# Prompt attention scores as three products of split halves instead of one full float32 product

## The reference, cut to what matters

```python
c_q, c_kv, kr_raw, g_a, x_b, g_b, q_m, g_m = split_cols(x @ w_in, EVEN_SPLITS)
q = (rms_norm(c_q, q_norm) @ w_uq).reshape(B, T, H_A, QK_NOPE + QK_ROPE)     # 8 heads, 64 + 32
q_lat = jnp.einsum('bthn,chn->bhtc', q[..., :QK_NOPE], w_uk)
q_rope = jnp.transpose(rope(q[..., QK_NOPE:], pos), (0, 2, 1, 3))
latent = rms_norm(c_kv, kv_norm)
k_rope = rope(kr_raw[:, :, None, :], pos)[:, :, 0, :]
...
s = (q_lat . latent + q_rope . k_rope) * MLA_SCALE       # causal, blocks of 128 queries
p = softmax(s);  o_lat = p @ latent;  y_a = o_lat @ w_uv
mixed = concatenate([y_a * silu(g_a), h_b * silu(g_b), y_m * silu(g_m)])   # h_b: RG-LRU, y_m: memory attention
```

## Time and profile before

| | us |
|---|---|
| median of 3 runs | 1392.4 |
| lowest and highest | 1391.83, 1393.7 |
| profiled execution, own time | 1393.73 |
| its span | 1392.1 |
| PE busy in the span | 1364.4 (98%) |
| DVE busy | 814.5 (59%) |
| ACT busy | 591.9 (43%) |
| mean granted clock of TensorE | 0.994 of full speed |

### The profile page before, as it was taken

How to read it: one execution, slowest core, us unless ns; L and a number is a source line. 1 busy time by engine, 2 the same in 40 slices (tenths; PEclk the granted TensorE clock), 3 DMA queues, 4 the chain that set the end, 5 groups by cost and what they waited for, 6 DMA issues and landing times.

```text
span 1392.1 us, 24975 instructions
## 1 busy us (share of the span) xinstructions
PE 1364.4 (98%) x10020; PEld 1236.3 (89%) x10020; DVE 814.5 (59%) x1541; ACT 591.9 (43%) x1062; POOL 116.9 (8%) x215
## 2 busy tenths in 40 slices
PE   9999999999999999999999999999999999999996
PEld 9988999787767667689998898999999999999996
DVE  4487753175675766756984344325444649545786
ACT  4169622156566565533552333115443135212453
POOL 1000000010001305600002000010000010000000
PEclk9999999999999999999999999999999999999998
DMA  6211133210003057745665311124334120124562
GB/s 215 63 31 46 31 112 103 75 43 14 1 1 124 15 144 224 204 146 181 211 201 188 107 31 43 61 62 66 61 61 115 31 107 31 48 68 154 172 217 94
DMA packets 59300, 135.77 MB, mean 98 GB/s; under 512 B 9001, under 2 KB 37898, under 8 KB 58418
## 3 DMA queue, kind: packets, MB, share of 16 engines
q1 hardware_dynamic: 48882, 112.45, 25.2%
q0 software_dynamic: 10160, 21.56, 6.5%
q10 hardware_dynamic: 144, 0.18, 0.0%
HBM read 120.65 MB, written 13.50 MB: 96 GB/s over the span
## 4 chain that ended last, share of the span: by engine, by line
PE 83%; DVE 7%; issue 5%; ACT 3%; POOLq 1%; DMA 0%; POOL 0%; DVEq 0%; ACTq 0%
PE ps L578 14%; PE ps L580 13%; PE ps L579 13%; PE ps L710 5%; PE ps L712 5%; PE ps L711 5%; PE ps L1153 3%; PE ps L1190 2%; PE ps L1165 2%; PE ps L1327 2%; PE ps L591 1%; PE ps L3278 1%; PE ps L3273 1%; DVE ln_sq L981 1%; DVE w_lo L526 1%
## 5 line engine op out<-in xcount | busy, mean ns | idle before, releaser
L578 PE MATMUL ps<-x_hi,w_hi 128*128 128x352 f32 x1288 | 425.7, 331 | 0.0
L580 PE MATMUL ps<-x_hi,w_lo 128*128 128x352 f32 x1288 | 415.0, 322 | 0.0
L579 PE MATMUL ps<-x_lo,w_hi 128*128 128x352 f32 x1288 | 414.5, 322 | 0.0
L578 PEld LDWEIGHTS ps<-x_hi,w_hi 128*128 128x128 f32 x1288 | 242.8, 189 | 9.7 <-issue 9.0
L579 PEld LDWEIGHTS ps<-x_lo,w_hi 128*128 128x128 f32 x1288 | 243.7, 189 | 1.0 <-issue 1.0
L580 PEld LDWEIGHTS ps<-x_hi,w_lo 128*128 128x128 f32 x1288 | 242.7, 188 | 0.0
L520 ACT ACTIVATE w_hi<-w_raw 128x1024 fp32r<-128x1024 f32 (+1 forms) x105 | 121.2, 1154 | 239.9 <-PE ps L580 132.3
L526 DVE TENSOR_TENSOR w_lo<-w_raw,w_hi 128x1024 fp32r<-128x1024 f32 (+1 forms) x105 | 141.1, 1344 | 61.9 <-ACT w_hi L520 61.5
L710 PE MATMUL ps<-mx_hi,w_hi 128*128 128x352 f32 x480 | 155.5, 324 | 0.3 <-issue 0.2
L712 PE MATMUL ps<-mx_hi,w_lo 128*128 128x352 f32 x480 | 154.5, 322 | 0.0
L711 PE MATMUL ps<-mx_lo,w_hi 128*128 128x352 f32 x480 | 154.0, 321 | 0.0
(11 more groups left out here) (515 smaller groups left out, 2003.0 us busy)
## 6 DMA issues: line engine op xcount, KB each, us to landing
w_raw<-in_w_out SPq DMA_DIRECT2D x48, 640.0 KB, 3.8
w_raw<-in_w_in SPq DMA_DIRECT2D x57, 512.0 KB, 3.6
page<-in_cache_mla SPq DMA_DIRECT2D x128, 128.0 KB, 2.5
kvs<-in_mem_cache SPq DMA_DIRECT2D x16, 512.0 KB, 4.8
x_res<-in_xT SPq DMA_DIRECT2D x24, 176.0 KB, 2.4
x<-x_next POOLq DMA_DIRECT2D x3, 1408.0 KB, 7.9
x_res<-x SPq DMA_DIRECT2D x24, 176.0 KB, 2.3
w_mem<-in_w_mem SPq DMA_DIRECT2D x2, 2048.0 KB, 10.6
```

Of the source, the lines that this page charges most:

```text
L578: pe.matmul(out, w_hi[:, (u + 1) % 2, kk], x_hi[:, k, chunk(c)], start=(k == 0), stop=False)
L579: pe.matmul(out, w_hi[:, (u + 1) % 2, kk], x_lo[:, k, chunk(c)], start=False, stop=False)
L580: mm = pe.matmul(out, w_lo[:, (u + 1) % 2, kk], x_hi[:, k, chunk(c)], start=False, stop=(k == KX - 1))
```

## The change

Scores are made of halves as the projections are. ScalarE rounds a unit's 128 columns of `qT` to `q_hi` (`query_hi`), VectorE subtracts (`query_lo`), and PE adds three products of type float32r. `query_hi` and `query_lo` of the units in `ISSUE[n+1]` stand in step n of their engines. The keys are kept as `kT_hi` and `kT_lo`. For the first pair VectorE makes `kT_lo` from PSUM; for the later pairs ScalarE first copies the whole piece into the buffer `rq` and makes `kT_hi` from there, and VectorE makes `kT_lo` from there. The rotated key is now made in input slots 60 and 61, with PSUM banks 5 to 7 as scratch, and PE's first pieces wait for it. `kT_lo` takes the place of `mx` tiles 4 to 7, which are written to memory after 233 us and read back behind the load of `w_uv`, ahead of the pages of the second half. Two small loads (`w_if`, the second mask) move to the end of the attention.

```diff
+        kT_hi = keep("kT_hi", [P, 4, T], F32R)
+        kT_lo = place("kT_lo", [P, 4, T], M0 + 4 * ROWS, F32R)
...
-                pe.wait_ge(rope_ready, u.h + 1)
+                pe.wait_ge(prep_ev, PAIR_PIECE[u.h // 2] + 5)
+                pe.wait_ge(kl_ready, 2 + 2 * u.h if u.h < 2 else KL_DONE[u.h // 2])
...
+                pe.wait_ge(ql_ready, HEAD_UNIT[n] + 1)
+                qh, ql = split_q_of(n)
+                w = u.nk // parts_of(u)
+                for a in range(parts_of(u)):
+                    s, ks = ps[:, u.bank + a, 0:w], (u, a * w, a * w + w)
+                    pe.matmul(s, qh, k_of(kT_hi, *ks), start=True, stop=False)
+                    pe.matmul(s, qh, k_of(kT_lo, *ks), start=False, stop=False)
+                    mm = pe.matmul(s, ql, k_of(kT_hi, *ks), start=False, stop=True)
...
+            def query_hi(n):
...
+                act.wait_ge(rope_ready, h + 1)
...
+                elif i >= 3:
+                    act.wait_ge(sc_ready, HEAD_AT[i - 3] + 1)
+                act.activation(split_q_of(n)[0], q_of(UNITS[n]), ACT.Copy).then_inc(qh_ready, 1)
...
             for n in range(len(UNITS)):
                 for k in ISSUE[n]:
                     maxima(k)
+                for k in ISSUE.get(n + 1, ()):
+                    query_lo(k)
                 invert(n)
                 if part_done_at(n) is not None:
                     into_mx(part_done_at(n))
...
+            def query_lo(n):
...
+                dve.wait_ge(qh_ready, HEAD_UNIT[n] + 1)
+                dve.tensor_tensor(lo, q_of(UNITS[n]), hi, ALU.subtract).then_inc(ql_ready, 1)
...
+                    if what == "k" and i >= N_FIRST:
+                        act.wait_ge(kl_ready, KL_DONE[p - 1] + (p == 2))
+                        act.activation(rq[:, cols], bank(b), ACT.Copy).then_inc(prep_ev, 1)
+                        act.wait_ge(prep_ev, i + 1)
+                        for r in range(2):
+                            act.activation(kT_hi[64 * r:64 * r + 64, s + r, cols], rq[64 * r:64 * r + 64, cols],
+                                           ACT.Copy).then_inc(kh_ready, 1)
+                        return
...
+        def dve_rope_key(dve, v, step):
+            part = ps[0:ROPE, 5:8, 0:CH]
+            if step == 0:
...
+                v.then(dve.stream_shuffle(raw, raw, swap))
+                v.then(dve.tensor_tensor(raw, raw, rope_sin[0:ROPE, :], ALU.mult))
+                dve.tensor_tensor(raw.rearrange("p (c n) -> p c n", c=NCH), raw.rearrange("p (c n) -> p c n", c=NCH),
+                                  part, ALU.add).then_inc(kr_ready, 1)
...
+            if s in (60, 61):
+                dve_rope_key(dve, v, s - 60)
...
+                sp.dma_start(mx[:, 4:8, :], mxd).then_inc(tbl_in, 16)
...
+            gp.wait_ge(lru_mul, 4)
+            gp.dma_start(mxd, mx[:, 4:8, :]).then_inc(spill, 16)
...
+            pe.wait_ge(kr_ready, 3)
             for i in range(N_FIRST - 1):
```

More of the change, by code:

```diff
@@ L242, in build @@
         rec2 = keep("rec2", [P, 2, P])
-        rec4 = [[place("rec4_00", [P, P], S0 + 7296), place("rec4_01", [P, P], S0 + 7808)],
-                [place("rec4_10", [P, P], X0 - 512), place("rec4_11", [P, P], at["rec2"])]]
-        assert at["rq"] <= S0 + 7296 and at["rec4_01"] <= S0 + 2 * ROWS
+        rec4 = [place("rec4_0", [P, P], X0 - 512), place("rec4_1", [P, P], at["rec2"])]
+        q_at = (at["kT_lo"], Z0 + 14 * ROWS + 4096, Z0 + 14 * ROWS + 4608, S0 + 7296, S0 + 7808, at["masks"] - 512)
+        q_hi = [place(f"q_hi{n}", [P, P], q_at[2 * n], F32R) for n in range(3)]
+        q_lo = [place(f"q_lo{n}", [P, P], q_at[2 * n + 1], F32R) for n in range(3)]
+        assert at["rq"] <= S0 + 7296 and at["q_lo1"] <= S0 + 7808 and at["q_hi0"] <= M0 + 8 * ROWS
         wh = place("wh", [P, 2, 7 * P], W0)
@@ L1108, in probs_of @@
             return probs[:, n % 2, 0:u.nk]
+        HEAD_AT = [n for n, u in enumerate(UNITS) if u.h is not None]
         FILLS, fill = {}, 0
@@ L1243, in act_attention, with dve_attention @@
                 evacuate(n)
-        def dve_attention(dve, v, between):
+        def dve_attention(dve, v, between, query_lo):
             def maxima(n):
@@ L1269, in invert @@
                     v.then(dve.reciprocal(mst[:, b, M_REC, :], mst[:, b, M_SUM, :]))
+                    last = max((g for g in range(PART_OF[n]) if PARTS[g].p is None), default=None)
+                    if last is not None:
+                        dve.wait_ge(o_ready, last + 1)
                     for t in range(2):
[L1271 removed]
+                        ins = dve.tensor_copy(rec4[t][:, :].rearrange("p (r d) -> p r d", r=2),
                                               mst[:, b, M_REC, 2 * t:2 * t + 2].unsqueeze(2).to_broadcast([P, 2, 64]))
@@ L3214, in _ @@
                 rope_sum(h)
-            rope_keys(2)
-            rope_keys(3)
-            v.settle()
-            dve_attention(dve, v, rope_at)
+            for h in range(2):
+                for i in (6, 7):
+                    keys_lo(i, h)
+                query_lo(h)
+            dve_attention(dve, v, rope_at, query_lo)
             dve_mla_sample(dve, v)
```

178 lines of the change are left out of this document (119 added, 59 removed).

## The result

The changed kernel takes 1433.5 us (median of 4 runs, 1432.04 to 1435.98) against 1392.3 us before: ratio 1.0296, 95% interval 1.0282 to 1.0311. It is 41 us slower where 27 had been forecast. The profiled execution lies at the median.

The account below looks back on a forecast made before the run. The prediction took PE to bound the kernel, busy 1364.4 of 1392.1 us. Its terms, -11.3 + 32.5 - 3 + 6 + 2.9 and 0 for memory, summed to +27.1 us: a median of 1419.5 us, range 1403 to 1433.

Parts of the forecast that it names:

- A: Attention scores on PE: three products of halves replace the full product, -11.3 us, bounds -9 to -12.
- B: Attention: PE waits for VectorE's `query_lo` before a unit's scores, late at 33 of 46 points, +32.5 us.
- C: Correction to the `query_lo` waits: VectorE catches up where its own backlog made it late, -3 us, between 0 and -10.
- D: New work on the keys, on VectorE and ScalarE, ahead of maxima and `query_lo`: +6 us, between 0 and +14.
- a rival: Attention: the clock falls after PE's many waits, adding 10 to 20 us, total 1430 to 1440 us; chance 0.09.
- E: Entry to the attention: PE waits for the rotated key, and the first scores start later, +2.9 us.
- F: Way of `mx` over memory, read back behind `w_uv` ahead of later pages: 0, range 0 to +5 us.
- the count of late points: Attention: `query_lo` comes too late for PE's scores at 33 of 46 points, VectorE in time at 13.
- The premise under A: Attention: PE binds, busy 215.43 of 222.20 us, so less PE work shortens it one for one if nothing takes its place.

Follow-up runs that it names:

- e4: Changed kernel plus useless transposes of the identity on PE ahead of its waits at units 9, 27, 51 and 52; 1424.5 us.
- e2: Changed kernel without `query_lo`; the third product takes `q_hi` again, so the scores lack a term; 1396.6 us.
- e3: Changed kernel with one full float32 score product again, without `query_hi` and `query_lo`, keys and entry kept as changed; 1400.2 us.
- e9: e7 with the product of `q_hi` and `kT_lo` left out, two products instead of three; 1399.0 us.
- e7: Changed kernel with `query_hi` and `query_lo` both one step earlier, two steps ahead, on their own engines; 1398.6 us.
- e8: e7 with PE's rotated-key wait at its second piece, pair 1's rotated-key copy and subtraction on GpSimd, two `rope_sum` two steps later; 1400.0 us.
- e10: e7 with PE's rotated-key wait at its second piece, `rope_sum` two steps later, GpSimd's zeros moved away from VectorE's copies; 1395.3 us.
- e12: e10 with all `query_lo` moved from VectorE to GpSimd, still two steps ahead; 1395.3 us.
- e11: Changed kernel with only GpSimd's zeros moved away from VectorE's copies of the rotated key; 1432.8 us.

## Why the prediction was wrong

The direction was right, and so was the mechanism of the waits; what the waits do to the clock was not, and the size of A was off. The 39.8 us of the two spans, by the steps of the prediction:

| step | forecast | measured | from |
|---|---|---|---|
| A, PE's work on scores | -11.3 | -6.4 | 8 sizes of unit, start to start |
| B, C, D, waits for `query_lo` | +35.5 | +36.8 | 32 places |
| slow clock in the stage | 0 (a rival) | +10.4 | windows |
| PE's other waits in the stage | 0 | -3.5 | 14.5 to 11.0, start to start |
| E, entry | +2.9 | +3.0 | 1.5 at the first piece, 1.5 to the first score |
| F, sample stage | 0 | +1.0 | 97.3 to 98.3 us |
| ahead of the first piece, behind the sample stage | 0 | +2.3, -1.6 | start of the same instructions |

They sum to 42.0, and the four of the stage to 37.3 where it grew by 35.0; this 2.2 us I can't assign. The slow clock is the least certain of them: filling the long waits in e4 took 7.0 us of it away and made the stage 6.1 us shorter. The -1.6 us in the last row is a stretch at the lower clock at 1105 us of the trace of before that the changed kernel's doesn't have.

**The step that failed is the sum's treatment of the clock.** It stood in the sum at nothing and was set apart as a rival of 0.09 at 1430 to 1440 us, with the argument that waits of this size had left the clock at 1.00 before. But before the longest wait in the stage was 1.2 us; the forecast's own list had waits of 2.3 us. The changed kernel's stage has 10.4 us of slow clock. e4 shows what the waits do: with the four longest filled, 7.0 us of it and 6.1 us of the stage are gone; in e2, without them, there is none, though PE waits 2.4 us for ScalarE there once. That the time lies in the rival's range is partly luck: the rival had a fifth of the stage at the lower level, the trace has a tenth (24 of 257 us), and A came out 4.9 us short. Also, the forecast spoke of "up to 2.3 us and more" but took no account of where the new work on the keys falls together with other work ahead of one `query_lo`: unit 9 (two key subtractions, the rotated key's copy and subtraction, two maxima) waited 3.9 us and unit 27 (two key subtractions and a `rope_sum` of 1.25 us) 3.0 us. D was spread over the steps in the forecast; these two places are where it gathers.

**A was mis-sized.** A unit of 1024 keys takes 1.47 us and not 1.35: 0.075 us is the first product behind other work of PE, with or without a wait, and the pace of 512 columns is 0.23 us and not 0.225. Over the eight sizes a head takes 6.9 us, not 6.3. Where the Trainium skill (TensorE: Matmul & The Clock Gate, Back-to-back issue gap) has 131 ns for a matmul of 512 columns in a stream, this trace shows 230 ns; its price would have been further off than mine.

**B, C and D held as a sum, to 1.3 us, and E to 0.1 us,** and so did the count of late points (32 for 33) and the first scores' 1.5 us behind the first piece. C and D can't be told apart in the traces, so that each was right is not shown. That the whole entry lies 2.3 us later than that is no part of the change's own work: 0.76 us are there after 24 us, and 1.5 us come at 119 to 124 us, where PE ran at the lower clock behind a wait of 1.81 us that left it alone in the kernel before (1.85 us, clock 1.00).

**The premise under A holds only so far.** "Less work on PE would shorten it one for one" was read from PE being busy 215 of 222 us. From e3 to e2, with the same keys and no `query_lo`, the three products do shorten the stage, by 6.2 us: A's saving is real. But e9 takes another 16 us from the products and the stage stays. PE was full before, but other work right beside it was nearly as long; the order of the program suggests the chain of scores, maxima on VectorE, exponentials and evacuation on ScalarE, and transposes. In the runs with the three products and almost no wait for `q_lo` in the stage (e2, e7, e8, e10, e12) it is 220.6 to 224.7 us long, and 224.1 us with two products (e9). The chain itself was not measured alone; which of its links would have to shrink stays open, as does whether a third lookahead would help.

## What to carry to other kernels

When a change puts an instruction of another engine between two steps of the engine that binds, its price is not its own 0.28 us but everything that stands ahead of it in that engine's queue: here 18 us of small subtractions made 37 us of waits, and preparing the operand one step earlier, in the same three buffers, took them away. Before a saving on a full engine is counted, ask how far it carries: with PE busy 97% of the stage the first 6 us came through (e3 to e2), and were used up by the work that makes the halves; the next 16 us did not (e7 to e9). And look at the longest single waits, not only at their sum, when deciding whether the clock belongs into the sum.

## What the runs showed of the hardware

**Clock.** Over the traces of all fourteen kernels, PE stood still for 2.9 us or more ahead of a product eight times, and the granted clock was lower behind it each time (0.50 to 0.69 in the 3 us after). Of 17 idle times of 2.0 to 2.7 us it fell behind 9, and of 30 of 1.5 to 1.75 us behind 9. It can fall without any: at 1105 us of the kernel before it did so while PE was busy all along, with small products of 32 and 128 columns just before. At one and the same place of the program, a wait of 1.81 to 1.86 us at 118 us, it fell in 9 of 14 traces; each time it did so it cost some 1.7 us, whatever the kernel. The Trainium skill (TensorE: Matmul & The Clock Gate, HAM oscillation — how this bites in real kernels) has a kernel in which each pause costs a stretch at the lower level. The four stretches of the stage here agree: 3 to 7 us at 1.2 GHz behind each of its four longest waits.

**VectorE and GpSimd.** A copy of 32 x 1024 on VectorE took 2.06 us beside GpSimd's zeros and 0.70 us without (e11); two-input operations of 1056 columns took 2.70 and 1.98 us beside GpSimd's subtraction and 1.23 and 1.26 without (e8 against e7). The Trainium skill (SBUF — State Buffer, Who interferes with whom) says that the two share a pair of ports: a VectorE copy in its fast mode and a GpSimd instruction hold it against each other for a whole instruction, and VectorE's two-input operations contend with GpSimd instructions that read. Both rows agree with it, and so does the other side: the zeros of `kT_lo`, written while the copies ran, took 2.34 us, and 1.81 us in e11 with no copy beside them. A subtraction of 128 columns took 0.50 us on GpSimd and 0.28 on VectorE, one of 64 x 512 1.37 and 0.69 us.
